# A wait ahead of four VectorE additions, for the roots that GpSimd makes, in a one-core decoder layer

## What is computed

```python
x = x + rms_norm(y, post_norm_mix)
h = rms_norm(x, pre_norm_mlp)
y = square(relu(h @ w_mlp_in)) @ w_mlp_out        # 1024 -> 4096 -> 1024
x = x + rms_norm(y, post_norm_mlp)

def rms_norm(x, w):
    return x * rsqrt(mean(x * x, axis=-1) + 1e-6) * w
```

## Time and profile before

| | |
|---|---|
| median of 3 runs | 742.15 us (741.41 to 743.57) |
| the profiled execution | 741.63 us |
| its span in the trace | 739.9 us |
| TensorE busy | 731.2 us, 99% of the span |
| VectorE busy | 520.0 us, 70% |
| ScalarE busy | 417.1 us, 56% |
| GpSimd busy | 308.3 us, 42% |
| mean granted TensorE clock | 0.999 of full speed |
| chain that ended last | TensorE 86%, GpSimd 5%, ScalarE 3%, VectorE 2% |

### The profile page before, as it was taken

One profiled execution on the slowest core, in us unless ns is written; L12 is line 12 of the kernel. 1 busy time (PEld: TensorE's weight loads), 2 busy tenths in 40 slices (PEclk: granted clock), 3 DMA queues, 4 the chain that ended last, 5 costly groups with the idle time before them and its releaser, 6 DMA issues.

```text
span 739.9 us, 12838 instructions
## 1 busy us (share of the span) xinstructions
PE 731.2 (99%) x4600; PEld 619.5 (84%) x4600; DVE 520.0 (70%) x783; ACT 417.1 (56%) x685; POOL 308.3 (42%) x289
## 2 busy tenths in 40 slices
PE   9999999999999999999999999999999999999996
PEld 7778778888887878788878978999999888888885
DVE  5897899981454545553892867878777977788785
ACT  6657842267653546535663745555555665565671
POOL 2348894546455854565527585222332000000002
PEclk9999999999999999999999999999999999999999
DMA  9557559987999799877783798688888598774652
GB/s 338 167 198 273 171 175 340 324 241 180 224 261 273 183 235 263 208 171 202 258 308 86 223 254 218 204 243 241 236 249 247 197 259 280 252 255 148 223 171 114
DMA packets 65768, 168.17 MB, mean 227 GB/s; under 512 B 7184, under 2 KB 7600, under 8 KB 63408
## 3 DMA queue, kind: packets, MB, share of 16 engines
q1 hardware_dynamic: 58000, 133.07, 52.3%
q0 software_dynamic: 7376, 34.08, 23.4%
q10 hardware_dynamic: 336, 0.28, 0.1%
HBM read 163.19 MB, written 67.13 MB: 311 GB/s over the span
## 4 chain that ended last, share of the span: by engine, by line
PE 86%; POOL 5%; ACT 3%; DVE 2%; DMA 1%; SPq 1%; issue 1%; POOLq 0%; ACTq 0%; DVEq 0%
PE bank L872 27%; PE bank L873 26%; PE bank L874 26%; POOL w_lo L2473 2%; POOL rsq L2461 2%; PE bank L1119 1%; PE bank L1142 1%; PE bank L1129 1%; DMA x_sb<-in_x 1%; PE bank L1083 1%; DVE qk_dn L1837 1%; PE bank L1047 1%; PE bank L1094 1%; ACT w_hi L1374 1%; PE bank L1181 0%
## 5 line engine op out<-in xcount | busy, mean ns | idle before, releaser
L2473 POOL TENSOR_TENSOR w_lo<-raw,w_hi 128x512 fp32r<-128x512 f32 x117 | 157.8, 1358 | 157.1 <-ACT w_hi L1374 155.3
L1374 ACT ACTIVATE w_hi<-raw 128x512 fp32r<-128x512 f32 (+2 forms) x202 | 137.7, 688 | 124.3 <-PE bank L874 104.1
L872 PE MATMUL bank<-h_hi,w_hi 128*128 128x512 f32 (+1 forms) x480 | 175.0, 365 | 1.5 <-POOL w_lo L2473 1.3
L873 PE MATMUL bank<-h_lo,w_hi 128*128 128x512 f32 (+1 forms) x480 | 170.3, 355 | 0.0
L874 PE MATMUL bank<-h_hi,w_lo 128*128 128x512 f32 (+1 forms) x480 | 170.2, 355 | 0.0
L872 PEld LDWEIGHTS bank<-h_hi,w_hi 128*128 128x128 f32 x480 | 90.7, 189 | 20.8 <-issue 4.5
L874 PEld LDWEIGHTS bank<-h_hi,w_lo 128*128 128x128 f32 x480 | 90.7, 189 | 13.1
L873 PEld LDWEIGHTS bank<-h_lo,w_hi 128*128 128x128 f32 x480 | 90.9, 189 | 11.2
L872 PE MATMUL bank<-ts_hi,w_hi 128*128 128x256 f32 x192 | 54.3, 283 | 0.0
L873 PE MATMUL bank<-ts_lo,w_hi 128*128 128x256 f32 x192 | 54.3, 283 | 0.0
L874 PE MATMUL bank<-ts_hi,w_lo 128*128 128x256 f32 x192 | 54.3, 283 | 0.0
(11 more groups left out here) (360 smaller groups left out, 1590.0 us busy)
## 6 DMA issues: line engine op xcount, KB each, us to landing
raw<-in_w_in SPq DMA_DIRECT2D x87, 256.0 KB, 4.6
t_in_sum<-in_w_mlp_in SPq DMA_DIRECT2D x9, 1024.0 KB, 6.8
raw<-in_w_mlp_in SPq DMA_DIRECT2D x30, 256.0 KB, 4.0
raw<-in_w_mlp_out SPq DMA_DIRECT2D x26, 256.0 KB, 2.9
raw<-t_sum SPq DMA_DIRECT2D x26, 256.0 KB, 3.7
raw_m<-t_in_sum SPq DMA_DIRECT2D x22, 256.0 KB, 4.3
raw_m<-in_w_mlp_in SPq DMA_DIRECT2D x20, 256.0 KB, 5.0
v_sum<-in_w_mlp_out POOLq DMA_DIRECT2D x4, 1024.0 KB, 9.5
```

Of the source, the lines that this page charges most:

```text
L872: pe.matmul(o, s_hi, m_hi, start=start, stop=False, skip_group_check=True)
L873: pe.matmul(o, s_hi, m_lo, start=False, stop=False, skip_group_check=True)
L1374: return a.activation(o, i_, ACT.Copy, scale=scale)
L2473: g.tensor_tensor(w_lo[:, u % 4, :], raw_of(u), w_hi[:, u % 4, :].bitcast(F32), ALU.subtract).then_inc(lo_ready, 1)
```

## The change

VectorE waits for `rs2_ready` ahead of the four additions. One line is added, and all else is as before, on every engine. On VectorE's list it stands behind the last instruction that makes `h_lo`.

```diff
@@ -2328,6 +2328,7 @@
                 if s == STEPS_IN - 1 and v_ in (12, 13):
                     w_low(v_ - 12, 1, v_ - 11)
 
+        v.wait_ge(rs2_ready, 1)
         for b in range(4):
             full_block(b)
         v.wait_ge(row_ready, 2)
```

## The result

| | before | changed |
|---|---|---|
| median of 17 runs | 741.82 us (741.01 to 743.57) | 744.70 us (742.85 to 745.68) |
| ratio | | 1.0032, 95% interval 1.0025 to 1.0038 |
| the profiled execution, its span | 741.63, 739.9 us | 744.27, 742.5 us |
| mean granted TensorE clock | 0.999 | 0.996 |

The changed kernel is slower, by 0.32% or 2.4 us with the interval from 1.9 to 2.8. That is just at the bound of 0.3%. The means of the two sets of 17 lie 2.4 us apart, as the ratio says, the medians 2.9. The forecast was +1.0 us.

What follows compares the result with a forecast made beforehand. TensorE, busy 99%, was taken to bound the kernel. Two pauses, 1.64 us, are traded for one of about 2.65: +1.0 on 742.15, rounded up to 743.2 us; range 741.7 to 744.3.

Steps and rivals of the forecast that it cites:

- The pauses before units 4 and 6 go: TensorE's waits for GpSimd's low parts of the first MLP weights, 0.42 and 1.22 us, vanish, putting TensorE 1.64 us ahead.
- The roots gain 2.06: GpSimd's two root operations, no longer disturbed by VectorE's additions, end at 428.98 instead of 431.04.
- GpSimd goes first by 0.02 us: When the roots end, near 429, GpSimd's split 6 starts ahead of VectorE's first addition and runs 429.06 to 430.35.
- Turns of 2.23: VectorE's additions alternate with GpSimd's splits 6 to 9, 2.23 us a pair; the last addition ends at 438.12.
- upper bound of 2.52: A turn without any overlap, 1.29 + 1.23 us; the last addition would end 1.0 us later, the sum +2.0.
- Unit 8 waits for the relus: TensorE could start unit 8 at 436.85 but gets VectorE's first two relus at 439.39; with restart, +1.0 us.
- The restart of 0.11 is all that the new pause costs beyond its length: At unit 8, TensorE's pause adds only a 0.11 us restart in the sum; nothing after it absorbs the loss.
- rival C: TensorE's idle pause before unit 8 lowers its clock, losing 1.5 us more: +2.5 us, 744.7; chance 0.06.
- Rival B: Additions after the roots cost only their own time, ending at 433.6; both pauses go: -1.64 us, 740.5; chance 0.07.

Runs made afterwards that it cites:

- the placement between the splits: Kernel before, with VectorE's first two additions waiting for unit 4's low part and the last two for unit 6's; 740.83 us, ratio 0.9989; repeated 740.47 us, 0.9983.

## Why the prediction was right or wrong

1. *The pauses before units 4 and 6 go.* Right: forecast 1.64 us ahead. The last matmul of unit 7 started at 436.43 - 423.29 = 13.14 after split 4, before at 438.26 - 423.44 = 14.82, so 1.68.
2. *The roots gain 2.06.* Right: 428.81 - 423.29 = 5.52 after split 4, before 431.04 - 423.44 = 7.60, so 2.08.
3. *GpSimd goes first by 0.02 us.* Right in the changed kernel (0.01), and shown to be what decides: with the order turned by a memset of 0.09 us, the loss is gone.
4. *Turns of 2.23.* Right: three turns and the first addition end at 437.95, forecast 438.12. The upper bound of 2.52 did not come; a pair overlaps by 0.3 us. The loser stands still for 1.1 us in either order (2.35 against 1.23 for the addition, 2.35 against 1.29 for the split). The Trainium skill (page "SBUF — State Buffer", section "SBUF: two separate sides") says that the first to start holds the shared port pair for its whole instruction and the other fully blocks. As to who waits, the trace agrees; as to the length, the overlap is more than that allows.
5. *Unit 8 waits for the relus.* Right: 2.55 behind its beat where 2.54 were forecast (439.39 - 436.85), and 0.87 later than before where 0.90 were (439.39 - 438.49).
6. *The restart of 0.11 is all that the new pause costs beyond its length.* **Wrong**, and this is the step that failed. The sum took 0.11 us for the restart, which the run with nine extra matmuls bears out (0.13), and nothing for the clock; the pause lowered TensorE's clock to 0.50, and that cost another 1.58. It was rival C, given 0.06, with its price of 1.5 close. I had leaned on the tail, where the clock stays at 1.00 in a stretch of 3.0 us without a matmul. That one observation showed that an idle TensorE can keep its clock that long; it did not show that it always does. In the changed kernel the pause was shorter, 2.4 us, and the fall came within 0.1 us of the first matmul behind it. Why the clock outlasts the longer idle stretch and not this one stays open.
7. *The number.* 743.2 was forecast, 744.7 measured, 0.4 above the range's upper end of 744.3. As a change, +1.0 was forecast, and +2.4 measured by the ratio. The late relus were sized to 0.1 us, the clock was left out of the range, and it is the larger half of the loss. As a ratio the loss straddles the 0.3% on which "same" and "slower" part, and 0.94 to 0.05 was too sure of it.

Rival B, that the turns don't last, is out by the 9.04 us of the four additions. Not settled is whether the clock falls in every execution of the changed kernel. Its 17 executions spread from 742.85 to 745.68, and one without the fall should lie near the 743.4 of the run with nine extra matmuls. The two fastest, 742.85 and 742.90, have a mean granted clock of 0.998 and not 0.996, but one of 744.82 has 1.000, so the clock of a whole execution doesn't sort them, and only one has a timeline. Over all 17 it averages 0.997, over the eleven with nine extra matmuls 0.998; a stretch of 3.4 us at half the clock would take 0.0023 off each, an estimate from the span and the slow stretch of the profile, so the averages don't settle it either.

## What to carry to other kernels

Work that looks free because its engine idles afterwards has a deadline: when it is moved, work out when it ends with what it then collides with, against the first instruction queued behind it, not only what it stops disturbing. Price a new pause of TensorE twice, by its length and by the clock that it may cost; here two short pauses (0.44 and 0.54) in place of the long one, or useless matmuls in it, kept the clock. And where two engines share a path, place the work between the operations on the critical path, and don't let a near-tie of two starts decide: here 0.02 us decided between no loss and 2.4 us, the larger part of it through the clock.

## What the runs showed that I had not expected

- Who starts first behind a common release went with the place of the wait. Ahead of the first addition, GpSimd started 0.01 to 0.02 us ahead of VectorE in all four traces with that wait and no memset. Ahead of the second or third addition it was 0.05 to 0.06 behind. VectorE began the first addition 0.10 to 0.11 behind the operation that released it, and a later one 0.03 to 0.04; the placement between the splits has both (424.26 to 424.36, and 430.66 to 430.70). One difference is on record: the first addition also waits for `t2_lo`, as the order of instructions in "The change" shows, and the later ones there have no wait of their own. Whether that is the 0.07 was not tried.
- The granted clock did not fall in the pause but with the restart: it is 1.00 up to 439.20 and 0.50 from 439.30.
- Splits of unit 4 start between 422.97 and 425.29 in the twelve traces, behind code that no experiment touched, and the second matrix's loop lost 0.17 us in one and 1.26 us in another. Medians of ten runs hide an effect of half a microsecond in this. A ruler between two instructions around the change gave the same number to 0.05 us in runs with the additions in the same place and no late relus (35.55, 35.57, 35.52; 36.86, 36.81), whether TensorE's wait stood or not.
